# Differential queries and keys by products of 512 columns, and another first table on ScalarE

## What is computed

```python
h = rmsnorm(x, norm_mix_g[i])
u = h @ w_in[i]
u_rwkv, u_attn, u_gate = jnp.split(u, [RWKV_COLS, RWKV_COLS + ATTN_COLS], axis=-1)
o_a = rwkv7_time_mix(u_rwkv, ...)   # tanh and sigmoid of low-rank columns; a recurrence over the tokens
o_b = diff_attention(u_attn, ...)
#   q, k, v = split(u_attn, 3); q = q * 64 ** -0.5; causal softmax of q k^T twice per head, the difference times v
g_a, g_b = jnp.split(jax.nn.sigmoid(u_gate), 2, axis=-1)
merged = g_a * (o_a @ w_proj_a[i]) + g_b * (o_b @ w_proj_b[i])
x = x + merged @ w_out[i]
```

## Time and profile before

| | us |
|---|---|
| median of three runs (1414.63 to 1416.10) | 1414.87 |
| the profiled execution | 1415.34 |
| its span, first to last instruction | 1413.40 |
| TensorE busy | 1406.8 |
| VectorE busy | 1179.5 |
| ScalarE busy | 819.2 |

### The profile page before, as it was taken

The page is one execution under the profiler, slowest core; times in us unless marked ns, Lnnn a source line. Parts: engine busy times, 40 slices in busy tenths (PEclk is TensorE's granted clock), DMA queues, the critical chain, the costliest instruction groups (busy, mean ns, idle before and its releaser), DMA issues.

```text
span 1413.4 us, 22918 instructions
## 1 busy us (share of the span) xinstructions
PE 1406.8 (100%) x9197; PEld 1197.1 (85%) x9197; DVE 1179.5 (83%) x1641; ACT 819.2 (58%) x1103; POOL 26.5 (2%) x93
## 2 busy tenths in 40 slices
PE   9999999999999999999999999999999999999999
PEld 8988778888888888889878888888888887888887
DVE  6876786898877898998868988988889798688897
ACT  7735474565447555555766665555555557665562
POOL 0000000000001100000000000000000000000000
PEclk9999999999999999999999999999999999999999
DMA  8441236555554555455434555545555453355543
GB/s 335 155 151 62 101 110 208 173 185 203 194 221 179 185 203 185 173 208 192 141 118 172 185 195 187 213 169 197 200 179 197 165 177 148 112 201 195 180 177 119
DMA packets 36105, 249.12 MB, mean 176 GB/s; under 512 B 4128, under 2 KB 4256, under 8 KB 6688
## 3 DMA queue, kind: packets, MB, share of 16 engines
q1 hardware_dynamic: 35712, 247.46, 49.4%
q10 hardware_dynamic: 288, 0.19, 0.1%
HBM read 246.59 MB, written 1.05 MB: 175 GB/s over the span
## 4 chain that ended last, share of the span: by engine, by line
PE 97%; DMA 1%; ACT 1%; DVE 0%; issue 0%; SPq 0%; DVEq 0%; ACTq 0%
PE ps L2219 24%; PE ps L2131 16%; PE ps L2133 15%; PE ps L2132 15%; PE ps L2226 13%; PE ps L2393 2%; PE ps L2203 1%; PE ps L2207 1%; PE ps L2209 1%; DMA raw<-ws 1%; PE ps L2307 1%; PE ps L2606 1%; PE ps L2586 1%; PE ps L2595 1%; PE ps L2378 0%; ACT hi L2649 0%
## 5 line engine op out<-in xcount | busy, mean ns | idle before, releaser
L3017 DVE TENSOR_TENSOR lo<-raw,hi 128x2048 fp32r<-128x2048 f32 (+1 forms) x230 | 525.0, 2283 | 60.3 <-ACT hi L2649 57.6
L2649 ACT CAST hi<-raw 128x2048 fp32r<-128x2048 f32 (+1 forms) x230 | 439.8, 1913 | 186.6 <-PE ps L2133 118.9
L2219 PE MATMUL ps<-h,hi 128*128 128x512 f32 x1504 | 359.0, 390 | 0.0
L2219 PEld LDWEIGHTS ps<-h,hi 128*128 128x128 f32 x1504 | 276.4, 188 | 52.5
L2131 PE MATMUL ps<-hi,a 128*128 128x512 f32 x516 | 205.0, 397 | 0.0
L2133 PE MATMUL ps<-hi,a 128*128 128x512 f32 x516 | 201.4, 390 | 0.0
L2132 PE MATMUL ps<-lo,a 128*128 128x512 f32 x516 | 201.2, 390 | 0.0
L2226 PEld LDWEIGHTS ps<-h,lo 128*128 128x128 f32 x1504 | 192.2, 190 | 7.9
L2226 PE MATMUL ps<-h,lo 128*128 128x256 f32 x1504 | 194.4, 282 | 0.0
L2846 ACT COPY a<-ps 128x256 f32<-128x256 f32 x208 | 76.1, 373 | 143.5 <-PE ps L2219 78.5
L2131 PEld LDWEIGHTS ps<-hi,a 128*128 128x128 f32 x516 | 96.9, 188 | 22.6 <-issue 2.4
(11 more groups left out here) (383 smaller groups left out, 1800.1 us busy)
## 6 DMA issues: line engine op xcount, KB each, us to landing
raw<-ws SPq DMA_DIRECT2D x229, 1024.0 KB, 4.8
X<-xin SPq DMA_DIRECT2D x8, 256.0 KB, 5.3
raw<-ws SPq DMA_DIRECT2D x2, 512.0 KB, 6.5
out<-X SPq DMA_DIRECT2D x4, 256.0 KB, 2.2
small<-small SPq DMA_DIRECT2D x1, 992.5 KB, 12.8
const<-const SPq DMA_DIRECT2D x1, 900.0 KB, 6.8
a<-row SPq DMA_DIRECT2D x1, 512.0 KB, 6.2
const<-const SPq DMA_DIRECT2D x1, 388.0 KB, 13.2
```

The source lines that it names most:

```text
L2219: t = e.matmul(b2(s["slots"][u]), wh[:, k, 128 * u:128 * u + 128], h2[:, k, :, :], start=k == 0, stop=last)
L2649: e.copy(hi[j % NSPL][:, n], raw[j % NRAW][:, n]).then_inc(hi_ready, 1)
L3017: e.tensor_tensor(lo[j % NSPL][:, n], raw[j % NRAW][:, n], hi[j % NSPL][:, n].bitcast(F), ALU.subtract).then_inc(lo_ready, 1)
```

## The change

The four pieces of differential queries and keys are multiplied by `wide_runs` instead of `cols_piece`. A new track `queries` takes each finished piece: ScalarE copies the two `HL` halves (`halves`), VectorE adds them to the `HH` halves and then scales in place (`dqk`), and a semaphore of its own tells `d_soft` that all four are there. The planner's estimate for `lora_in` goes from 3.4 to 0.85 us, and the table that ScalarE loads at the start is the set with sigmoid and tanh.

```diff
--- before.py
+++ after.py
@@ -34,6 +34,7 @@
 ROOT = 3.0
 RWKV_ORDER = (1536, 512, 768, 0, 256, 1024, 1280)
 LN_EXP = "natural_log_exp_and_others"
+SIGMOIDS = "sigmoid_and_others"
 
 
 
@@ -255,6 +256,7 @@
         rstd_ready = Sig(sem("rstd_ready"))
         factors = Sig(sem("token_factors"))
         diag_ready = Sig(sem("diag_ready"))
+        scaled_v = Sig(sem("queries_scaled"))
         c_part = Sig(sem("c_part"))
         c_ready = Sig(sem("c_ready"))
         rwkv_a = Named(sem("rwkv_act"))
@@ -1271,7 +1273,7 @@
             yield from have(1)
             yield "act"
             rwkv_a.mark("lora_in")
-            emit("lora_in", act=3.4)
+            emit("lora_in", act=0.85)
             lora = []
             for c2 in range(2):
                 yield "pe"
@@ -1603,7 +1605,7 @@
                 state["gates"] = True
 
         def diff():
-            while "vd" not in state or "bonus" not in state:
+            while "vd" not in state or "bonus" not in state or "dk" not in state:
                 yield None
             yield "dve"
             emit("lam", dve=0.5, act=0.2, us=state["bonus"], v=diff_v.add(), v_a=diff_a.add())
@@ -1662,6 +1664,23 @@
                 state["ob_v"] = diff_v.n
             state["ob"] = pv
 
+        to_scale = []
+
+        def queries():
+
+            for n in range(4):
+                while len(to_scale) <= n:
+                    yield None
+                c, sl, other, at = to_scale[n]
+                yield "act", at
+                emit("halves", act=0.7, slots=(other, sl), qk="dq" if n < 2 else "dk", n=2 * n % 4, v=[half_a.add() for _ in range(2)])
+                halves = script[-1]["v"]
+                yield "dve"
+                emit("dqk", dve=1.4, slots=(other, sl), halves=halves, n=(c - 1792) // 128, v=scaled_v.add())
+                for x in (other, sl):
+                    give(x)
+            state["dk"] = scaled_v.n
+
         to_shift = []
         early = []
 
@@ -1696,14 +1715,16 @@
                 else:
                     yield from cols_piece("w_in", 0, c, "h", nm.h_needs, shift)
 
-            def dq(sl, c, nxt):
-                emit("dqk", dve=0.7, slot=sl, n=(c - 1792) // 128)
-                if nxt:
-                    emit_lo(nxt)
-                state["dk"] = sl
+            def dq(sl, c, nxt, other):
+                to_scale.append((c, sl, other, cur[0]))
+                emit_lo(nxt)
+                return True
+
+            def begin(sl, c, u):
+                pass
 
             for c in range(1792, 2816, 256):
-                yield from cols_piece("w_in", 0, c, "h", nm.h_needs, dq)
+                yield from wide_runs("w_in", 0, c, nm.h_needs, begin, dq)
 
             def vd(sl, b, h):
                 emit("d_v", act=0.7, slot=sl, b=b, rstd=nm.rstd)
@@ -1743,7 +1764,7 @@
                 yield from rows_mat("w_proj_b", 0, 4, 512 * half, 512, "ob", lambda k, b: (diff_v.sem, state["ob_v"]),
                                     pb(half))
 
-        weave([shifts(), rwkv_decays(), rwkv_keys(), (rwkv_chain(), LEAD), (rwkv_block(0), LEAD), (rwkv_block(1), LEAD),
+        weave([shifts(), queries(), rwkv_decays(), rwkv_keys(), (rwkv_chain(), LEAD), (rwkv_block(0), LEAD), (rwkv_block(1), LEAD),
                (rwkv_out(0), LEAD), (rwkv_out(1), LEAD), (diff(), LEAD + 2.0), gates()],
               [mixers_fill(nm)])
 
@@ -2494,7 +2515,7 @@
                     for z in s["slots"]:
                         claim(z)
                     if h == 0:
-                        read_out(state["dk"])
+                        e.wait_ge(scaled_v.sem, state["dk"])
                     for a0, a1 in ((0, 128), (128, 384)):
                         for c, z in enumerate(s["slots"]):
                             t = e.matmul(banks[z.b][:, a0:a1], qT[half(c), h, a0:a0 + 128], kTt[half(c), h, 0:a1 - a0],
@@ -2607,6 +2628,10 @@
                                          ETb[s["i"]][:, p, c0:c0 + 256 - q0], start=b == 0, stop=b == 1)
                     t.then_inc(full[sl.b], 1)
 
+        def halves_of(s):
+
+            return {"dq": qT, "dk": kTt}[s["qk"]][:, s["n"]:s["n"] + 2, :]
+
         def scalar_program(e):
             own = [0]
 
@@ -2677,7 +2702,7 @@
                     e.activation(banks[sl.b][:, :], X[:, b, 512 * h:512 * h + 512], ACT.Square,
                                  accum_out=st[:, i:i + 1]).then_inc(x_squared.sem, 1)
                 elif kind == "table":
-                    e.preload_act_table_set(LN_EXP)
+                    e.preload_act_table_set(SIGMOIDS)
                 elif kind == "f_gain":
                     e.wait_ge(row_in, 16)
                     e.activation(frow2[:, :], frow[:, :], ACT.Square).then_inc(fin_a.sem, 1)
@@ -2690,6 +2715,11 @@
                                  accum_out=st[:, i:i + 1]).then_inc(x_squared.sem, 1)
 
 
+                elif kind == "halves":
+                    to = halves_of(s)
+                    for u, x in enumerate(s["slots"]):
+                        ready(x)
+                        e.copy(to[:, u, :], b2(x)[:, 1, :]).then_inc(half_a.sem, 1)
                 elif kind == "shift_old":
                     read_out(sl)
                     c, u_ = s["c"] // 128, ub[s["i"]]
@@ -2830,7 +2860,7 @@
                 elif kind == "gate_sig":
                     part = {"A": gA, "B": gB}[s["g"]][:, :, 512 * s["half"]:512 * s["half"] + 512]
                     if s["table"]:
-                        e.preload_act_table_set("sigmoid_and_others")
+                        e.preload_act_table_set(SIGMOIDS)
                     read_out(sl)
                     e.activation(part, part, ACT.Sigmoid).then_inc(gate_a.sem, 1)
                 elif kind == "m_turn":
@@ -2978,6 +3008,15 @@
                                        top[:, 0:1])
                 return e.tensor_tensor_reduce(E[:, 128:384], banks[sl.b][:, 128:384], bias[:, 128:384], 1.0, LOWEST,
                                               ALU.add, ALU.max, top[:, 1:2])
+
+            def meet_halves(s, to):
+
+                for u, x in enumerate(s["slots"]):
+                    e.wait_ge(half_a.sem, s["halves"][u])
+                    e.tensor_tensor(to[:, u, :], b2(x)[:, 0, :], to[:, u, :], ALU.add).then_inc(free[x.b], 1)
+                for x in s["slots"]:
+                    read_out(x)
+                return to
 
             def add_halves(s, to):
 
@@ -3354,14 +3393,9 @@
                     e.tensor_tensor(obL[:, h, :], oT[:, :], obH[:, h, :].bitcast(F), ALU.subtract).then_inc(diff_v.sem, 1)
                 elif kind == "dqk":
                     n = s["n"]
-                    ready(sl)
-                    if n < 4:
-                        e.scalar_tensor_tensor(qT[:, n:n + 2, :], b2(sl), 0.125, RB2, ALU.mult,
-                                               ALU.mult).then_inc(free[sl.b], 1)
-                    else:
-                        e.tensor_tensor(kTt[:, n - 4:n - 2, :], b2(sl), RB2, ALU.mult).then_inc(free[sl.b], 1)
-
-
+                    t = meet_halves(s, halves_of({"qk": "dq" if n < 4 else "dk", "n": n % 4}))
+                    t = e.scalar_tensor_tensor(t, t, 0.125 if n < 4 else 1.0, RB2, ALU.mult, ALU.mult)
+                    t.then_inc(scaled_v.sem, 1)
                 elif kind == "gate_in":
                     b, o = s["b"], slice(512 * s["half"], 512 * s["half"] + 512)
                     e.wait_ge(rstd_ready.sem, s["rstd"])
```

## The result

The changed kernel takes **1418.34 us** (1417.44 to 1419.09) where the kernel before, run beside it, takes 1415.25: a ratio of 1.0022, 95% interval 1.0014 to 1.0029. It is slower by 3.1 us; the forecast was 1.13 us faster, in a range that ended at 1417.5. The profiled execution took 1417.88 us, its span is 1416.1.

What follows compares the result with a forecast made beforehand. TensorE was taken as the bound, busy 1406.8 of 1413.4 us. Pieces 0.82 plus first table 0.31 gave 1.13 us, so 1414.87 - 1.13 = 1413.7 us; range 1411.5 to 1417.5, forecast's chance 0.52.

Steps and rivals of the forecast that it cites:

- The pieces: Four query and key pieces on TensorE: 512-column products take 5.555 us a piece instead of 5.76, saving 0.82 us.
- Insertions: Four small chain products that cut the pieces move to their borders or behind: taken as nothing, bounds +/-0.76 us.
- The first table: ScalarE's two table loads in lora_in, 1.28 us each, go; TensorE's wait at lora shrinks, saving 0.31 us.
- TensorE feels only the wait: At lora: of 2.56 us of loads removed, TensorE gains only its step's excess, 0.52 against 0.21: 0.31 us.
- The added work beside TensorE: At the pieces: 3.0 us of ScalarE copies hidden, 3.36 us more on VectorE about covered by its idle time.
- the 3.36 us: VectorE's added work over the four pieces: two additions and one multiplication come, one multiplication goes, 0.84 us a piece.
- rival A: The chain comes late: delayed scores and last shift idle TensorE ahead of proj_a, 7.12 us in full, 1420.9; chance 0.17.
- So the rest of the kernel keeps its work: Outside the changed stage: four extra runs leave the later ones' alternation as it was; no cost booked.
- the rivals: Chain comes late, 1420.9, chance 0.17; small waits vanish too, 1412.7, 0.21; change does less than it says, 1414.4, 0.10.

Runs made afterwards that it cites:

- the two runs: Changed kernel, lora_in's old estimate, 128 tiny instructions, the pieces' scaling on GpSimd: 1416.44 us; the same with VectorE's estimate cut to 0.75: 1416.63 us.

## Why the prediction was wrong

**The pieces: right.** 5.57 us where 5.555 was said, so 0.77 us is won where 0.82 was. The price by the earlier trace rows held, with one score between the third and the fourth. The estimate beside it from the Trainium skill ("TensorE: Matmul & The Clock Gate", section "Back-to-back issue gap"), 0.17 (0.16 by the page's cycles), did not.

**Insertions: right.** Taken as nothing, within 0.76 either way; some 0.32 us were won, by the difference that is left.

**The first table: wrong in sign.** That both loads go was right, also that no drain showed. The step that failed is "TensorE feels only the wait", with its bounds of 0 to 0.31. The text itself named the way ("If the new order places lora too early again, nothing is gained here"), and priced it at no gain where it is a loss of 1.05 us (trace), 0.9 in the medians. The diff has the number that decides it, 0.85 for 3.4: an estimate that is true of ScalarE's two operations, but not of the addition on VectorE ahead of the tanh, which ends 0.95 us after ScalarE is free. With the estimate put back, lora starts 0.21 us after the product ahead of it (30.15 to 30.36), so the 0.31 of the loads alone was right.

**The added work beside TensorE: right for the changed kernel, not by itself.** The scaled queries were due before 90 us and their last multiplication starts at 93.10, still far ahead of d_soft at 111.78; the last low half starts at 209.89, later than the 209 set as a bound, but only because all of TensorE is 2.9 us later. Behind lora's wait the 3.36 us cost nothing. With that wait gone, VectorE takes some 0.5 us back (0.59 and 0.48 where 0.32 and 0.24 are usual). That is rival A in small, at another place than it named: at the scores of 82 to 85 us, not ahead of proj_a. The cover had been counted as a sum over 28 us (4.03 idle against 3.36), where it has to be there at each due operation.

**"So the rest of the kernel keeps its work": the step that failed.** It does keep its work, to the product, and still takes 2.9 us longer. I had booked 64 fewer products as fewer starts and nothing else. They also take 128 instructions out of TensorE's stream, which moves every later instruction by half a packet of 256. All four breaks are at one position in the count by 256; the same 128 instructions make the kernel before 3.6 us slower (in the trace 4.5, of which 0.94 is not breaks) and the changed one 2.9 us faster. None of the rivals was of this kind, which is why the range ended below the result.

By the Trainium skill ("Runtime: NRT & Kernel Launch", section "Instruction fetch mechanics") each engine's sequencer streams its program in 16 KiB blocks of 256 instructions, and crossing a boundary is mostly hidden behind the pace of issue. Size and number agree with the 74 packets of 16.4 KB in the profile; "mostly hidden" does not hold where 56 products take 1.04 us.

**What stays open.** That TensorE waited for a packet is inferred from three things: the position, the packet that starts 2.2 to 2.9 us ahead of each restart, and the lack of anything else awaited. No record names the wait. The length of a block does not decide whether it breaks: 256 instructions that take 3.54 us in the kernel before (100.77 to 104.31) have no break, while in the changed kernel those from 98.98 to 103.58 have one, 3.68 us without it, and the forecast by block length failed (without the warm-up, 1417.0 instead of 1414.5 to 1415.1).

What tells these two apart is when the packet of that block starts. Counted in order, each packet of the queue starts near the beginning of one block (4.7 us before to 7.3 us after, in all traces): 0.78 us into the first of the two (101.55) and 2.35 us into the second (101.33). At all 1,019 borders in the fourteen traces the first instruction of the next block, number 193 modulo 256, starts 2.23 us or more after that packet; the one just ahead of it, number 192, starts as early as 0.90 us after it. The first of the two blocks ended 2.76 us after its packet and ran on; the second started number 192 after 1.34 us (102.67) and stood still until 2.26. So a break comes where a packet starts late in a short block. What makes it start late in one layout and not in the other was not found.

No version here beats the kernel before by more than its interval. The best with all of the computation is the changed kernel with lora's old estimate and the 128 tiny instructions, 1415.08 beside 1415.37.

## What to carry to other kernels

When an edit changes the number of instructions of the engine that sets the time, compare the traces behind it too, where nothing was edited: a wait for "issue" in a run of short instructions, at the same number modulo 256 and some 2.2 us or more behind an instruction packet, is the layout of the program and not the edit, and some instructions added where the engine waits anyway tell the two apart. An estimate in a planner has to cover what the operation waits for and not only what its own engine does; 0.85 for 3.4 moved TensorE 24 products too early. And cover is to be counted up to each operation that is due, not over a stage.

## What the runs showed of the hardware that was not expected

- TensorE stood still for 0.3 to 1.3 us at a time in runs of small products (64 columns, 56 in 1.04 us), always at number 193 or 194 modulo 256 as the trace counts its instructions. In all clear cases the restart came 2.2 to 2.9 us after the start of a 16 KB packet that itself took 0.9 to 1.3 us; at none of the 1,019 borders in all traces did number 193 start less than 2.23 us after the packet of its turn.
- VectorE's operation of 128x12 took 1.25 us instead of 0.17 while GpSimd multiplied 128x512 from SBUF, and ended with it; GpSimd's own four took 1.3 to 3.4 us in the two runs, against 0.69 for the same size on VectorE. By the Trainium skill ("SBUF — State Buffer", section "SBUF: two separate sides") the two engines share a pair of ports that one of them holds for a whole instruction, on VectorE's side among others for an operation with two inputs in SBUF while GpSimd reads SBUF. The two rows agree with that: VectorE's has two such inputs, and GpSimd's 2.32 us also span the VectorE operation that started 0.05 us before it and took 1.22.
- 256 tiny instructions in the warm-up cost 2.8 us, 128 cost 0.9 in the kernel before: TensorE's wait for its first operand had room for fewer than these.
